# Two transformer blocks on one core: ranks and selection ahead of the gates, and a different order of the last group's weights

## The reference

```python
g_p, g_idx = lax.top_k(softmax(hf @ rg_w + rg_b), 1)          # one of 4 groups of 8 experts
e_p, e_idx = lax.top_k(softmax(e_sel), 2)                     # 2 experts in it
gates = g_p * (e_p / sum(e_p))
...
y = (silu(hb @ w1[e]) * (hb @ w3[e])) @ w2[e]                 # hb: the expert's tokens
out = zeros.at[slot_tok].add(y * slot_gate)
x = x + g2 * out;  return rmsnorm(x, final_g)
```

## Time and profile before

| | |
|---|---|
| median of 3 runs | 1416.24 us (1415.18 to 1419.88) |
| the profiled execution's own time | 1421.21 us |
| its span | 1419.4 us |
| TensorE matmul busy | 1193.8 us (84%) |
| VectorE, ScalarE busy | 593.0 us (42%), 435.9 us (31%) |
| moved by DMA | 362.98 MB, mean 256 GB/s |
| mean granted TensorE clock | 0.929 of full |

### The profile page before, as it was taken

How to read it: one execution, slowest core, us unless ns; L and a number is a source line. 1 busy time by engine, 2 the same in 40 slices (tenths; PEclk the granted TensorE clock), 3 DMA queues, 4 the chain that set the end, 5 groups by cost and what they waited for, 6 DMA issues and landing times.

```text
span 1419.4 us, 19224 instructions
## 1 busy us (share of the span) xinstructions
PE 1193.8 (84%) x8218; PEld 872.1 (61%) x8218; DVE 593.0 (42%) x971; ACT 435.9 (31%) x689; POOL 16.1 (1%) x32
## 2 busy tenths in 40 slices
PE   5999989999999999999999989897663655647675
PEld 5998756599887787599988767654331322213221
DVE  4678413576643666366643567822100101001011
ACT  4653320344433686354432522623010000000001
POOL 3000000000000000000000000000000000000000
PEclk9999989999999999999999999999787878868798
DMA  8352659354554555154455634568999999999995
GB/s 268 133 192 106 215 204 353 129 178 179 191 210 163 200 178 179 60 178 178 178 188 183 208 120 159 206 238 343 428 428 427 428 428 428 428 428 428 428 424 210
DMA packets 100656, 362.98 MB, mean 256 GB/s; under 512 B 7481, under 2 KB 10900, under 8 KB 88676
## 3 DMA queue, kind: packets, MB, share of 16 engines
q1 hardware_dynamic: 98544, 357.64, 65.1%
q0 software_dynamic: 1680, 4.10, 1.1%
q10 hardware_dynamic: 356, 0.13, 0.0%
HBM read 360.81 MB, written 1.05 MB: 255 GB/s over the span
## 4 chain that ended last, share of the span: by engine, by line
PE 64%; DMA 20%; DVE 3%; ACT 2%; issue 2%; SPq 1%; DVEq 0%; ACTq 0%
PE bank L932 34%; DMA arena<-in_exp_w 20%; PE bank L628 7%; PE bank L1046 3%; PE bank L904 3%; PE bank L1574 2%; PE bank L1239 2%; PE bank L871 2%; PE bank L914 2%; PE bank L600 1%; PE bank L1256 1%; SPq L2831 1%; PE bank L1270 1%; PE bank L1284 1%; DVE low_w L1737 1%
## 5 line engine op out<-in xcount | busy, mean ns | idle before, releaser
L628 PE MATMUL bank<-arena 128*32 128x512 f32 x880 | 185.8, 692 | 76.4 <-DMA arena<-in_exp_w 75.4
L1737 DVE TENSOR_TENSOR low_w<-ring,split_high 128x2048 fp32r<-128x2048 f32 x84 | 189.6, 2288 | 104.3 <-ACT split_high L2428 104.2
L932 PE MATMUL bank<-turned_high,low_w 128*128 128x256 f32 x720 | 204.3, 284 | 0.0
L2428 ACT ACTIVATE split_high<-ring 128x2048 fp32r<-128x2048 f32 x84 | 157.8, 1916 | 136.9 <-DMA ring<-in_w_down 66.9
L628 PE MATMUL bank<-ring,arena 128*32 128x512 f32 x528 | 92.2, 683 | 77.3 <-DMA arena<-in_exp_w 77.3
L932 PE MATMUL bank<-turned_high,split_high 128*128 128x256 f32 x512 | 145.9, 285 | 3.0 <-DVE turned_low L1752 3.0
L932 PE MATMUL bank<-turned_low,split_high 128*128 128x256 f32 x512 | 144.9, 283 | 0.0
L932 PEld LDWEIGHTS bank<-turned_high,low_w 128*128 128x128 f32 x720 | 138.8, 193 | 0.0
L628 PEld LDWEIGHTS bank<-arena 128*32 128x32 f32 x880 | 48.3, 125 | 138.7 <-issue 138.7
L786 DVE TENSOR_TENSOR arena<-arena,bank 128x512 f32<-128x512 f32 x8 | 5.5, 687 | 291.2 <-PE bank L628 253.9
L628 PEld LDWEIGHTS bank<-ring,arena 128*32 128x32 f32 x528 | 26.3, 124 | 139.6 <-issue 139.6
(11 more groups left out here) (457 smaller groups left out, 1928.9 us busy)
## 6 DMA issues: line engine op xcount, KB each, us to landing
arena<-in_exp_w SPq DMA_DIRECT2D x51, 2048.0 KB, 23.3
ring<-in_exp_w SPq DMA_DIRECT2D x33, 2048.0 KB, 19.4
ring<-in_w_up SPq DMA_DIRECT2D x16, 2048.0 KB, 8.9
ring<-in_w_down SPq DMA_DIRECT2D x16, 2048.0 KB, 7.7
ring<-in_mod_w SPq DMA_DIRECT2D x12, 2048.0 KB, 8.4
ring<-in_w_in_ar SPq DMA_DIRECT2D x7, 2048.0 KB, 8.4
ring<-in_w_qkv SPq DMA_DIRECT2D x6, 2048.0 KB, 8.0
arena<-in_exp_w SPq DMA_DIRECT2D x18, 512.0 KB, 11.6
```

Of the source, the lines that this page charges most:

```text
L628: last = nc.tensor.matmul(mb[bank][strip(e), :], act[:, k, strip(e)], w[e][:, k, cols], start=(k == 0), stop=(k == n_k - 1), skip_group_ch ...
L932: last = mm(dst, *pair, start=(start and i == 0), stop=(stop and i == 2))
L1737: v.tensor_tensor(low_of(name, s), half_of(slot(name), name, s), high_of(name, s).bitcast(F32), ALU.subtract).then_inc(sem("split_low"), 1)
L2428: nc.scalar.activation(high_of(name, s), half_of(slot(name), name, s), ACT.Copy)\
```

## The change

1. *Ranks first.* On VectorE the ranks, `choose` and the largest count now come right after `chosen_ready`; the gates come behind them, with a count of their own, `gates_ready`. The ranks and the largest count have a bank each. The empty first filling of `mb[0]` is 32 columns wide where it was 512.
2. *First product on four blocks.* TensorE waits only for ScalarE's lower four blocks before the first product; for VectorE's upper four it waits at block 4. `turn_select` of group 0 stands between the first and the second product.
3. *ScalarE* scales the tokens (`normed`) before it loads the table of exponentials; it was the other way round.
4. *SyncE at the start:* unit 7 goes out right behind unit 4 (`scaled` has moved to another place), the pieces for `hT` before `mix2_added`.
5. *Early places* now hold 11 of the 16 pieces (two blocks of one expert, 512 KB) of the last group's *second* weights.
6. *The end:* after the third product of the last but one group come the 5 second pieces that are left and 11 pieces of the third weights, after the last group's first product the other 5. All 16 third pieces go by rows (block m of four experts), and TensorE multiplies a row when it has landed.
7. Three semaphores of the convolution are one, counted in the same order (1, 2 / 3 / 4, 5).

```diff
@@ -405,7 +405,7 @@
...
-        scaled = half(48)
+        scaled = half(0)
...
@@ -433,6 +433,11 @@
...
+        pieces = [(i, e) for i in range(EC) for e in range(IN_GROUP)]
+        free_places = iter([blocks(moe_slot[s], EC)[:, i, :] for s in range(MOE_SLOTS) for i in range(EC)])
+        late_place = {at: next(free_places) for at in pieces if at not in early_place}
+        third_place = {at: next(free_places) for at in pieces}
+        thirds_first = EC * IN_GROUP - len(late_place)
 
 
         ssq, ssq2, rstd, rstd2, flags = tiny(NT), tiny(NT), tiny(NT), tiny(NT), tiny(24)
@@ -624,6 +629,8 @@
...
+                if by_pairs and k == n_k // 2:
+                    pe.wait_ge(moe_freed[3], 1)
...
@@ -634,6 +641,10 @@
...
+                if at_start and bank == 1:
+                    pe.wait_ge(banks.freed[5], banks.taken[5])
+                    pe.wait_ge(sem("gates_ready"), 1)
+                    turn_select(0, 0)
...
@@ -653,22 +664,16 @@
...
+            def last_products():
+
+                for m in range(EC):
+                    pe.wait_ge(sem(f"row_landed{m}"), 16 * IN_GROUP)
                     for n in range(2):
                         for e in range(IN_GROUP):
-                            w = blocks(moe_slot[unit_slot(unit + e)], EC)[:, m, :] if e in late else early_place[(m, e)]
-                            last = mm(mb[2 + n][strip(e), :], actT_m[:, m, strip(e)], w[:, n * 512:(n + 1) * 512],
-                                      start=(m == order[0]), stop=(m == order[-1]), skip_group_check=True)
-                        if m == order[-1]:
+                            last = mm(mb[2 + n][strip(e), :], actT_m[:, m, strip(e)],
+                                      third_place[(m, e)][:, n * 512:(n + 1) * 512],
+                                      start=(m == 0), stop=(m == EC - 1), skip_group_check=True)
+                        if m == EC - 1:
...
@@ -704,22 +709,18 @@
...
-                at = unit + IN_GROUP
-                w = [blocks(moe_slot[unit_slot(at + e)], KC) for e in range(IN_GROUP)]
-                for part in range(2):
-                    if part:
-                        pe.wait_ge(sem("moe_late_landed"), 16 * IN_GROUP * EC)
-                    else:
-                        for e in range(IN_GROUP):
-                            pe.wait_ge(moe_landed[unit_slot(at + e)], unit_landed(turn, at + e))
-                    for k in range(part * KC // 2, (part + 1) * KC // 2):
-                        for e in range(IN_GROUP):
-                            done = mm(mb[1][strip(e), :], gathered_k[:, k, strip(e)], w[e][:, k, :], start=(k == 0),
-                                      stop=(k == KC - 1), skip_group_check=True)
+                pe.wait_ge(sem("early_landed"), 16 * len(early_place))
+                pe.wait_ge(sem("moe_late_landed"), 16 * (IN_GROUP * (EC - 1) + len(late_place)))
+                for k in range(KC):
+                    for e in range(IN_GROUP):
+                        place = early_place.get((k // 2, e))
+                        w = blocks(late_place[(k // 2, e)] if place is None else place, 2)
+                        done = mm(mb[1][strip(e), :], gathered_k[:, k, strip(e)], w[:, k % 2, :], start=(k == 0),
+                                  stop=(k == KC - 1), skip_group_check=True)
                 done.then_inc(moe_full[1], 1)
                 turn_act(p2, q)
                 pe.wait_ge(moe_freed[0], filled(p2, q, SECOND))
-                last_products(turn, unit + 2 * IN_GROUP)
+                last_products()
...
@@ -1668,19 +1669,19 @@
...
-            mm(bank.ap[:, N_EXP:2 * N_EXP], ones, chosen[:, 0, :], start=False, stop=True)
-            for t in range(NT):
-                last = mm(bank.ap[:, 2 * N_EXP:3 * N_EXP], ones, chosen[:, t, :], start=(t == 0), stop=(t == 1))
+            mm(bank.ap[:, N_EXP:2 * N_EXP], ones, chosen[:, 0, :], start=False, stop=True).then_inc(bank.full, 1)
+            bank = banks.take(pe, "most")
+            for t in range(NT):
+                last = mm(bank.ap[:, 0:N_EXP], ones, chosen[:, t, :], start=(t == 0), stop=(t == 1))
             last.then_inc(bank.full, 1)
-            for b in range(4, 8):
+            for b in (4, 6, 7):
                 pe.wait_ge(banks.freed[b], banks.taken[b])
-            mm(mb[0], zeros, finite, start=True, stop=True, skip_group_check=True).then_inc(moe_full[0], 1)
+            mm(mb[0][:, 0:SLOTS_OF], zeros, finite[:, 0:SLOTS_OF], start=True, stop=True, skip_group_check=True)\
+                .then_inc(moe_full[0], 1)
             pe.wait_ge(sem("normed"), NT * 3)
             pe.wait_ge(sem("selected"), 1)
             gather(0)
-            turn_select(0, 0)
-            for b in (2, 3):
-                pe.wait_ge(moe_freed[b], 1)
+            pe.wait_ge(moe_freed[2], 1)
...
@@ -2364,6 +2365,19 @@
...
+            far = e_all.rearrange("p t g e -> p t (g e)")
+            v.tensor_scalar(far, chosen, -float(1 << 20), float(1 << 20), ALU.mult, ALU.add).then_inc(sem("dve_moe"), 1)
+            dve.wait_ge(sem("dve_moe"), 3)
+            bank = banks.read(dve, "rank")
+            v.tensor_tensor(rank[:, :, 0:N_EXP], bank.ap[:, 0:2 * N_EXP].rearrange("p (t n) -> p t n", t=NT), far,
+                            ALU.add).then_inc(bank.freed, 1)
+            banks.wait_read(dve, "rank")
+            choose(0, 0)
+            bank = banks.read(dve, "most")
+            v.tensor_reduce(most, bank.ap[:, 0:N_EXP], AX.X, ALU.max).then_inc(bank.freed, 1)
+            banks.wait_read(dve, "most")
+            v.tensor_copy(most_int[:, :], most).then_inc(sem("most_ready"), 1)
+            v.memset(flags[:, 20:21], 0.0).then_inc(moe_freed[0], 1)
             dve.wait_ge(sem("route_exp"), 2)
...
@@ -2371,16 +2385,8 @@
...
-            step(v.tensor_tensor(by_group(gates), h1.unsqueeze(2).to_broadcast([P, NT, 4, 8]), in_group, ALU.mult))
-            bank = banks.read(dve, "rank")
-            step(v.tensor_scalar(chosen, chosen, -float(1 << 20), float(1 << 20), ALU.mult, ALU.add))
-            step(v.tensor_reduce(most, bank.ap[:, 2 * N_EXP:3 * N_EXP], AX.X, ALU.max))
-            v.tensor_tensor(rank[:, :, 0:N_EXP], bank.ap[:, 0:2 * N_EXP].rearrange("p (t n) -> p t n", t=NT), chosen,
-                            ALU.add).then_inc(bank.freed, 1)
-            banks.wait_read(dve, "rank")
-            choose(0, 0)
-            v.tensor_copy(most_int[:, :], most).then_inc(sem("most_ready"), 1)
-            v.memset(flags[:, 20:21], 0.0).then_inc(moe_freed[0], 1)
+            v.tensor_tensor(by_group(gates), h1.unsqueeze(2).to_broadcast([P, NT, 4, 8]), in_group, ALU.mult)\
+                .then_inc(sem("gates_ready"), 1)
...
@@ -2779,11 +2785,11 @@
...
-            step(s.activation(warm, eps_col, ACT.Exp))
             act.wait_ge(sem("rstd_ready"), 1)
             for t in range(NT):
                 s.activation(blocks(xn3[:, t, :], KC), x3[:, t, :].rearrange("p (q k) -> p k q", k=KC), ACT.Copy,
                              scale=rstd[:, t:t + 1]).then_inc(sem("normed"), 1)
+            step(s.activation(warm, eps_col, ACT.Exp))
...
@@ -2832,18 +2838,17 @@
...
-            def load_half(part, e):
-                at, ks = unit_slot(a_turn - 2 * IN_GROUP + e), slice(part * KC // 2, (part + 1) * KC // 2)
-                sp.dma_start(blocks(moe_slot[at], KC)[:, ks, :], pkn(sources[1][N_EXP - IN_GROUP + e])[:, ks, :])\
-                    .then_inc(moe_landed[at] if part == 0 else sem("moe_late_landed"), 16)
-
-            def load_piece(m, e, place, landed_as):
+            def load_second(k2, e, place, landed_as):
+                src = pkn(sources[1][N_EXP - IN_GROUP + e])[:, 2 * k2:2 * k2 + 2, :]
+                sp.dma_start(blocks(place, 2), src).then_inc(sem(landed_as), 16)
+
+            def load_third(m, e):
...
@@ -2865,12 +2870,13 @@
...
             load_unit(0, 4)
+            load_unit(0, 7)
             for c in range(2):
                 sp.wait_ge(*unit_read[("w_out2", c)])
                 load_unit(0, 5 + c)
+            load_early((3, 0), (3, 1))
             sp.wait_ge(sem("mix2_added"), 1)
-            load_unit(0, 7)
-            load_early((2, 3), (3, 0), (3, 1))
+            load_early((2, 3))
             sp.wait_ge(sem("x_taken"), 1)
             sp.wait_ge(sem("normed"), NT * 3)
             load_early((3, 2), (3, 3))
@@ -2926,15 +2932,13 @@
...
-                for part in range(2):
-                    for e in range(IN_GROUP):
-                        load_half(part, e)
+                for at, place in late_place.items():
+                    load_second(*at, place, "moe_late_landed")
+                for at in pieces[:thirds_first]:
+                    load_third(*at)
                 sp.wait_ge(moe_full[0], filled(2 * GROUPS_A_TURN * turns, first_left // UNITS_A_GROUP, FIRST))
-                for m in range(EC):
-                    for e in range(IN_GROUP):
-                        if (m, e) not in early_place:
```

(4 more changed lines are left out.)

31 lines of the change are left out of this document (11 added, 20 removed).

## The result

| | before | after |
|---|---|---|
| median of 5 runs each | 1417.49 us (1415.18 to 1420.86) | 1408.56 us (1406.74 to 1409.93) |
| ratio of the times | | 0.9936 [0.9912, 0.9961] |
| span of the profiled execution | 1419.4 us | 1406.8 us |
| mean granted TensorE clock | 0.929 | 0.933 |
| moved by DMA | 362.98 MB | 362.98 MB |

A forecast was written before the change was run, and what follows sets the result against it. DMA engines, full from 982 us, bound the kernel; only that stretch's start and what follows its last bytes count. A 9.7 us gain less 1.0 for clock is 8.7: from 1416.24 to 1407.5 us, range 1403.8 to 1411.5.

The forecast's parts named there:

- Ranks before gates: VectorE reads the ranks sooner after the choice and a narrower first filling removes a wait: gather starts 1.4 us earlier.
- The gather: TensorE's gather from 967.5 meets the half-clock stretch where it stood and ends at 973.1, not at 974.27.
- Four blocks: TensorE's first product follows the gather at once, at 973.1 where it was 975.77; `pair_read` comes 2.7 us earlier.
- Rival B: TensorE's first pair is no earlier, so only the end gains: 6.0 us, 1410.2 us; chance 12%.
- Unit 7: Sending it and the `hT` pieces earlier gains nothing alone; without it 0.7 us or more of the start's gain is lost.
- The pieces: At the end, 8.39 MB of halves sent as 16 smaller pieces move at 410, not 419 GB/s: 0.5 us more.
- Rival A: Late pieces move at 279 GB/s, turning the gain into a loss of 3.9 us, 1420.1 us; chance 5%.
- Behind the last bytes: Second product runs unwaiting, TensorE waits 2.3 us for the last row; third product ends at 1400.3, not 1410.05.
- The clock at the end: TensorE may fall to half clock after waiting for the last row: 1.0 us allowed of 0 to 4.6.
- the last bytes come at 1400.6 - 2.7 + 0.5: End of the DMA queue: earlier start takes off 2.7 us, smaller pieces add 0.5, so last bytes come at 1398.4.
- 0.15 (landing to start): Time from the last row's landing to TensorE's start on it in the third product, taken as 0.15 us.
- One sign of being wrong: The prediction would be wrong if the DMA rate from 1372 us to the end is under 400 GB/s.

The follow-up runs named there:

- ranks late: The change with the gates' instructions again ahead of the ranks on VectorE; 1410.11 us, ratio 0.9961 to the kernel before.
- end alone: Parts 5 to 7 of the change on the kernel before, run twice: 1412.54 and 1411.30 us, ratios 0.9973 and 0.9971.
- start alone: Parts 1 to 4 and 7 of the change on the kernel before, run twice: 1417.30 and 1413.85 us, ratios 1.0008 and 0.9986.
- change again: The change measured and profiled a second time with no edit; 1408.54 us, ratio 0.9941 to the kernel before.

## Why the prediction was right

It said 1407.5 and the median is 1408.56, inside the forecast's own 1406 to 1410; against the runs of before beside it, 8.9 us where 8.7 were summed. That the two come so close is partly luck: terms that were off by 1 to 2 us cancel. Point by point:

- *Ranks before gates*: 1.4 us predicted, 1.2 shown by ranks late; VectorE's read comes 0.85 us behind the choice (within 0.9). Right.
- *The gather*: a slow stretch that stays in its place was taken, and cost 0.2 of the 1.4 us. In the change it didn't come (3.81 us), which gave 1.6 us more; other profiles have it or not with the same code. What I had read as a property of the place was one execution's luck, and stands as such in both kernels.
- *Four blocks*: the product at once behind the gather instead of 1.5 us later, as predicted. With the ranks, 2.7 predicted, **3.0 measured** between profiles with a gather at full clock. Rival B (the start does not move) is refuted as to the first piece by every profile. As to the time, the change lies 3.6 ± 2.0 us under the end alone, but the start alone looks like B.
- *Unit 7*: nothing by itself, 0.7 us or more lost without it. In the profiles 0.5 to 0.9, if the ragged end is taken off; the times don't resolve it, nor the 1 to 3 us expected before its run.
- *The pieces*: 0.5 us predicted, 0.5 measured at 409 GB/s. Right. Rival A is out.
- *Behind the last bytes*: the second product without a wait, the last row alone behind the last landing. The 11 to 13 us to the end are 11.4 and 12.9 from the landing, 11.9 and 13.5 from the end of the bytes in the bins, which is how the prediction's 18.8 was counted. Right in the main. The wait for the last row was 0.55 us and not 2.3, since half clock took 1.8 of it from rows 0 to 2.
- *The clock at the end*: 1.0 us allowed, of 0 to 4.6. The change's two profiles show 0 and 1.6, and so do the other profiles with this end: 1.5 to 1.6 in five of eight, a mean of 1.0. The upper bound was not met: of the four sums of the scatter only two pieces (1.14 us at full clock) are on the path; all four at half would have been 3.6 more, not 2.8.
- **The step that failed** is "the last bytes come at 1400.6 - 2.7 + 0.5". From the first piece to the end of the bytes in the bins it should have been 422.9 + 0.5 = 423.4 us; it is 424.8 and 424.9. The term held the mean rate alone and took the end of the queue as even as in the one profile of before. In both profiles of the change the slowest of the 16 engines works on alone for 1.0 us more; some 0.4 of the rest is not explained. Beside it, "0.15 (landing to start)" is some 0.55 us, since a transfer counts as landed 0.5 us after its last bytes. That is 1.9 us against the end; with no clock lost, where 1.0 was allowed, it gave 4.9 us in its profile where 8.7 - 2.7 = 6.0 were summed. Over the profiles with the new end it gives 3.4 (change again: ragged end, half clock) to 6.7 us (ranks late: even end, full clock). The start's 0.3 us more and the scatter of the medians covered the difference.

Of the signs named in the prediction, the first two and the second product's missing wait hold, in distances: VectorE's read, and the first product at the gather's end, 5.5 us behind the choice where 7.4 was forecast (nearly all the gather's full clock). Their moments, near 973 and 975, are 968.1 and 970.1, since the choice also came 3.0 us earlier. TensorE's last wait is 0.55 us and not some 2, and the share was full to 1391.5 us, not 1398. Of those 6.5 us, 3.0 are the earlier choice, 1.9 the start beyond its forecast, 1.6 the tail. One sign of being wrong came true as it was worded: the rate from 1372 to the last landing is 361 GB/s, under 400. But the tail is in that mean, and the same 23.4 us ahead of before's last landing have 387; to 1390 it is 408. The sign could not tell slow pieces from a tail.

## What to carry to other kernels

When a queue of transfers bounds a stage, ask what is still to do behind its last byte, and order the transfers so that only the smallest last step is; then price the landing of the slowest of the DMA engines too, since it was hidden behind other work until then, and price it from several executions (idle for 1.2 to 2.7 us of the last 4 here). A slow-clock stretch seen in one profile is a sample: read a second execution of the same kernel before it becomes a term, and measure parts by marks inside the profile (choice to first piece), which tell 1 us apart where runs that scatter by 3 us do not. Parts that add up in the profiles may not add up in the times; say so, and don't choose the pair that fits.

## What was unexpected of the hardware

- The clock falls at other moments in executions of one kernel. The gather of before takes 3.7 or 5.4 us, the last row of the change 1.92 or 3.30; the same code brings the choice at 961.1 or 965.6. Among the executions of one kernel, taken over all kernels here, the time falls by 0.93 us for each 0.001 of mean granted clock.
- The 16 DMA engines finish up to 4 us apart at the end of a full queue, with 0.33 to 0.70 of their time used in the last 4 us. The start alone has both ends of this range in its two profiles, and nothing in the order of the last pieces explains which.
- Transfers of 512 KB, one behind another, moved at 409 GB/s, those of 2048 KB at 428.
- A transfer counts as landed some 0.5 us after its last bytes in the bins (1394.9 and 1395.43 in the change).
